# Gathered rows of an expert-choice layer: sample rows fetched for two experts at a time, and their transposes set between the down matmuls

## What is computed

```python
logits = jnp.einsum('nd,de->en', hf, w_router)
aff = jax.nn.softmax(logits, axis=0)
gate, idx = lax.top_k(aff, cap)          # cap = 128 prompt rows, 64 sample rows
xg = hf[idx]
a = jnp.einsum('ecd,edf->ecf', xg, w_gate)
b = jnp.einsum('ecd,edf->ecf', xg, w_up)
out = jnp.einsum('ecf,efd->ecd', jax.nn.silu(a) * b, w_down) * gate[..., None]
y = jnp.zeros_like(hf).at[idx.reshape(-1)].add(out.reshape(-1, D))
```

## Time and profile before

| | |
|---|---|
| time, median of three executions | 2801.92 us (2797.81 to 2806.22) |
| profiled execution, span from the first to the last instruction | 2798.9 us |
| TensorE matmuls busy | 2615.8 us, 93% |
| VectorE busy | 1852.2 us, 66% |
| ScalarE busy | 1398.5 us, 50% |
| GpSimd busy | 391.0 us, 14% |
| mean granted TensorE clock | 0.966 |

### The profile page before, as it was taken

How to read it: one execution, slowest core, us unless ns; L and a number is a source line. 1 busy time by engine, 2 the same in 40 slices (tenths; PEclk the granted TensorE clock), 3 DMA queues, 4 the chain that set the end, 5 groups by cost and what they waited for, 6 DMA issues and landing times.

```text
span 2798.9 us, 41956 instructions
## 1 busy us (share of the span) xinstructions
PE 2615.8 (93%) x15956; PEld 2371.6 (85%) x15956; DVE 1852.2 (66%) x2211; ACT 1398.5 (50%) x1751; POOL 391.0 (14%) x344
## 2 busy tenths in 40 slices
PE   6979789997995599999999999999999999999997
PEld 5877678986784599898898998989989899898996
DVE  4876889986435566576665766756657566575664
ACT  4224355666312255465564554645546455465553
POOL 2081793000000101010010100101101011010000
PEclk8999999999997799999999999999999999999998
DMA  4112000002233468687686876868768678686773
GB/s 137 41 45 85 16 1 1 1 1 90 100 113 105 134 220 248 212 255 220 228 249 210 260 220 223 252 210 256 229 216 254 210 239 245 216 257 209 236 241 110
DMA packets 347982, 475.45 MB, mean 170 GB/s; under 512 B 10112, under 2 KB 301312, under 8 KB 347776
## 3 DMA queue, kind: packets, MB, share of 16 engines
q1 hardware_dynamic: 340736, 449.22, 49.7%
q0 software_dynamic: 7168, 25.17, 3.8%
HBM read 449.19 MB, written 25.17 MB: 169 GB/s over the span
## 4 chain that ended last, share of the span: by engine, by line
PE 87%; DVE 5%; POOL 3%; ACT 2%; issue 2%; DMA 1%; ACTq 0%; POOLq 0%; DVEq 0%
PE psum L1385 29%; PE psum L1387 13%; PE psum L1149 8%; PE psum L1151 8%; PE psum L1150 8%; PE psum L1263 5%; PE psum L1402 4%; PE psum L1403 4%; PE psum L1250 2%; PE psum L1238 2%; PE psum L1368 1%; POOL qn L448 1%; DVE wi_lo L811 1%; PE psum L1369 1%; PE psum L1339 1%
## 5 line engine op out<-in xcount | busy, mean ns | idle before, releaser
L1069 DVE TENSOR_TENSOR w_lo<-raw,w_hi 128x2048 fp32r<-128x2048 f32 x384 | 880.0, 2292 | 517.6 <-ACT w_hi L689 515.7
L1385 PE MATMUL psum<-xgT,w_hi 128*128 128x384 f32 x4096 | 1167.9, 359 | 3.4 <-issue 3.4
L1387 PE MATMUL psum<-xgT,w_lo 128*128 128x192 f32 x4096 | 1026.1, 251 | 0.0
L689 ACT CAST w_hi<-raw 128x2048 fp32r<-128x2048 f32 x384 | 733.3, 1910 | 356.8 <-PE psum L1403 356.8
L1387 PEld LDWEIGHTS psum<-xgT,w_lo 128*128 128x128 f32 x4096 | 783.4, 191 | 0.7
L1385 PEld LDWEIGHTS psum<-xgT,w_hi 128*128 128x128 f32 x4096 | 770.0, 188 | 4.2 <-issue 3.5
L486 POOL DMA_INDIRECT out_dram<-o_p,put_p x16 | 25.7, 1609 | 1568.7 <-ACT o_s L728 1568.7
L784 DVE SCALAR_TENSOR_TENSOR conv<-conv,colp 128x1024 f32<-128x1024 f32 (+1 forms) x210 | 234.0, 1114 | 4.0
L1149 PE MATMUL psum<-w_hi,hid_st 128*128 128x512 f32 x512 | 207.7, 406 | 0.0
L1151 PE MATMUL psum<-w_hi,hid_st 128*128 128x512 f32 x512 | 205.8, 402 | 0.0
L1150 PE MATMUL psum<-w_lo,hid_st 128*128 128x512 f32 x512 | 205.7, 402 | 0.0
(11 more groups left out here) (186 smaller groups left out, 3544.0 us busy)
## 6 DMA issues: line engine op xcount, KB each, us to landing
raw<-in_w_gate_dram SPq DMA_DIRECT2D x128, 1024.0 KB, 5.4
raw<-in_w_up_dram SPq DMA_DIRECT2D x128, 1024.0 KB, 5.4
raw<-in_w_down_dram SPq DMA_DIRECT2D x128, 1024.0 KB, 5.0
wi_raw<-in_w_in_dram SPq DMA_DIRECT2D x56, 256.0 KB, 3.8
out_dram<-x SPq DMA_DIRECT2D x12, 512.0 KB, 2.6
h_rows<-h SPq DMA_DIRECT2D x12, 512.0 KB, 2.8
xin<-in_x_prompt_dram SPq DMA_DIRECT2D x8, 512.0 KB, 3.6
wo_raw<-in_w_out_dram SPq DMA_DIRECT2D x8, 512.0 KB, 6.4
```

The lines of the kernel that those rows point to most:

```text
L689: act.copy(w_hi[:, j % SPLIT_SLOTS, :], raw[:, j % RAW_SLOTS, :]).then_inc(e_hi, 1)
L1069: dve.tensor_tensor(w_lo[:, j % SPLIT_SLOTS, :], raw[:, j % RAW_SLOTS, :], w_hi[:, j % SPLIT_SLOTS, :].bitcast(F32), ALU.subtract).then_in ...
L1385: pe.matmul(bank[:, 0:2 * CAP], w_hi[:, slot, w0:w0 + P], xgT[:, k, :], start=(k == 0), stop=False, skip_group_check=True)
L1387: last = pe.matmul(bank[:, 0:CAP], w_lo[:, slot, w0:w0 + P], xgT[:, k, 0:CAP], start=False, stop=(k == KD - 1), skip_group_check=True)
```

## The change

Sample rows are gathered for experts 2i and 2i+1 together: `rows_sg` and `cur_sg` hold 128 row numbers, `xg_s` is 128 rows high, and one indirect DMA (`gather_pair`) serves two experts. Prompt rows are gathered for each expert as before. `xgT` has a half for each expert of the pair. A turn into an odd expert transposes the eight prompt blocks alone; a turn into an even expert transposes eight prompt blocks and eight sample blocks of 128x128, which hold the rows of both experts of the pair. On TensorE the transposes of a turn stand singly or in twos behind each group of five down matmuls, over chunks 17 and 18, and the waits for the gathered rows stand ahead of chunk 17's matmuls. ScalarE and VectorE do their part behind step 21 in place of 20; in turns into even experts it is two instructions each. To treat the two kinds of expert apart, the loops of ScalarE, VectorE, GpSimd and TensorE now hold two experts and run 7 times.

```diff
+TURN_AT, TURNED_AT = 17, 21
...
-            xg_s = in_region(re_, "xg_s", [CAP_S, D], F32)
+            xg_s = in_region(re_, "xg_s", [2 * CAP_S, D], F32)
...
-            xgT = in_region(re_, "xgT", [P, KD, 2 * CAP], F32R)
+            xgT = in_region(re_, "xgT", [P, 2, KD, 2 * CAP], F32R)
...
+            gather_pair(0)
+            with pool.Fori(0, NE // 2 - 1) as i:
+                pool.wait_ge(xg_T, 2 * i + 1)
+                gather(2 * i + 1)
+                gather_pair(i + 1)
+                scatter(2 * i)
+                pool.wait_ge(xg_T, 2 * i + 2)
+                gather(2 * i + 2)
+                scatter(2 * i + 1)
...
-            def gathered_high(e):
+            def gathered_high(e, half):
 
                 act.wait_ge(xg_T, e + 1)
-                act.copy(xgT[:, :, 0:CAP].rearrange("p (a b) c -> p a b c", a=4),
-                         psum[:, 0:4, 0:2 * CAP].rearrange("p a (b c) -> p a b c", b=2)).then_inc(xg_h, 1)
+                last = act.copy(xgT[:, half, :, 0:CAP_P], gathered_prompt())
+                if half == 0:
+                    last = act.copy(xgT[:, :, :, CAP_P:CAP], gathered_sample())
+                last.then_inc(xg_h, 1)
...
-            def gathered_T(e):
-
-                pe.wait_ge(gathered, 32 * e + 32)
+            def turn_ready(e, i):
+
+                pe.wait_ge(gathered, 16 * e + 16)
+                if i is not None:
+                    pe.wait_ge(gathered_s, 16 * i + 16)
                 pe.wait_ge(g_sum, e * PAIRS)
                 pe.wait_ge(u_sum, e * PAIRS)
-                for k in range(KD):
-                    c0 = k % 2 * CAP
-                    pe.transpose(psum[:, k // 2, c0:c0 + CAP_P], xg_p[:, k * P:(k + 1) * P], ident[:, :])
-                    last = pe.transpose(psum[:, k // 2, c0 + CAP_P:c0 + CAP], xg_s[:, k * P:(k + 1) * P],
-                                        ident[0:CAP_S, 0:CAP_S])
-                last.then_inc(xg_T, 1)
...
+            def turn_block(k, with_sample):
+
+                last = pe.transpose(gathered_prompt()[:, k, :], xg_p[:, k * P:(k + 1) * P], ident[:, :])
+                if with_sample:
+                    last = pe.transpose(psum[:, 2 + k // 4, k % 4 * P:(k % 4 + 1) * P], xg_s[:, k * P:(k + 1) * P], ident[:, :])
+                return last
...
+                        if turn is not None and TURN_AT <= j < TURN_AT + 2:
+                            k = 4 * (j - TURN_AT) + 2 * i + half
+                            turned = turn_block(k, turn == 0)
+                            if k == KD - 1:
+                                turned.then_inc(xg_T, 1)
...
+            with pe.Fori(0, NE // 2 - 1) as i:
+                late(2 * i, 0, 1)
+                early(2 * i + 1, 1)
+                late(2 * i + 1, 1, 0, i + 1)
+                early(2 * i + 2, 0)
+            late(NE - 2, 0, 1)
+            early(NE - 1, 1)
+            late(NE - 1, 1, None)
```

More of the change, by code:

```diff
@@ L739, in step, with late, expert @@
                     hid_high(e, c // 2)
-            def late(e, last):
+            def late(e, turn):
                 for j in range(TURN, EC):
                     step(e, j)
-                    if j == 20 and not last:
-                        gathered_high(e + 1)
-            act.sem_inc(o_ok, 1)
-            act.wait_ge(proj, TILES)
-            for j in range(SPLIT_SLOTS):
-                step(0, j, first=True)
[L751 to L755, removed]
+                    if j == TURNED_AT and turn is not None:
+                        gathered_high(e + 1, turn)
+            def expert(e, turn):
+                late(e, turn)
                 for j in range(TURN):
@@ L760, in _ @@
                 out_rows(e)
-            late(NE - 1, True)
+            act.sem_inc(o_ok, 1)
+            act.wait_ge(proj, TILES)
+            for j in range(SPLIT_SLOTS):
+                step(0, j, first=True)
+            gathered_high(0, 0)
+            for j in range(SPLIT_SLOTS, TURN):
+                step(0, j)
+            with act.Fori(0, NE // 2 - 1) as i:
+                expert(2 * i, 1)
+                expert(2 * i + 1, 0)
+            expert(NE - 2, 1)
+            late(NE - 1, None)
             out_low(NE - 1)
@@ L1119, in step, with late, expert @@
                     hid_low(e, c // 2)
-            def late(e, last):
+            def late(e, turn):
                 for j in range(TURN, EC):
                     step(e, j)
[L1124 to L1134, removed]
+                    if j == TURNED_AT and turn is not None:
+                        gathered_low(e + 1, turn)
+            def expert(e, turn):
+                late(e, turn)
                 gates_of(e)
@@ L1139, in _ @@
                         out_add(e)
-            late(NE - 1, True)
+            dve.sem_inc(o_add, 1)
+            for j in range(SPLIT_SLOTS):
+                step(0, j)
+            gathered_low(0, 0)
+            for j in range(SPLIT_SLOTS, TURN):
+                step(0, j)
+            with dve.Fori(0, NE // 2 - 1) as i:
+                expert(2 * i, 1)
+                expert(2 * i + 1, 0)
+            expert(NE - 2, 1)
+            late(NE - 1, None)
             gates_of(NE - 1)
@@ L1373, in chunk @@
-            def chunk(e, j):
-                slot = j % SPLIT_SLOTS
-                pe.wait_ge(e_lo, e * EC + (j + 1))
[L1376 to L1403, removed]
-                last.then_inc(e_used, 1)
@@ new lines, in down @@
+            def down(e, j, turn=None, pair=None):
+                slot, jj = j % SPLIT_SLOTS, j - 2 * PAIRS
+                pe.wait_ge(e_lo, e * EC + (j + 1))
+                if jj == 0:
+                    pe.wait_ge(o_ok, 2 * e + 1)
+                pe.wait_ge(h_lo, 2 * (e * PAIRS + (jj + 1)))
+                if turn is not None and j == TURN_AT:
+                    turn_ready(e + 1, pair)
+                for i in range(2):
+                    st = hid_st[:, 2 * jj + i, :]
+                    first, end = jj == 0 and i == 0, j == EC - 1 and i == 1
+                    for half in range(2):
+                        w0 = i * D + half * 512
+                        hi, lo = w_hi[:, slot, w0:w0 + 512], w_lo[:, slot, w0:w0 + 512]
+                        product3(psum[:, 4 + half, :], st[:, 0:CAP_P], st[:, CAP + CAP_S:2 * CAP], hi, lo, first, end)
+                        both = st[:, CAP_P:CAP + CAP_S]
+                        pe.matmul(psum[:, 6 + half, :], both, hi, start=first, stop=False)
+                        last = pe.matmul(psum[:, 6 + half, :], both, lo, start=False, stop=end)
+                        if turn is not None and TURN_AT <= j < TURN_AT + 2:
[3 more added lines that the diff above has]
+                                turned.then_inc(xg_T, 1)
+                last.then_inc(e_used, 1)
@@ new lines, in early, with late @@
+            def early(e, half):
+                for j in range(TURN):
+                    gate_up(e, half, j)
+            def late(e, half, turn, pair=None):
+                for j in range(TURN, 2 * PAIRS):
+                    gate_up(e, half, j)
+                for j in range(2 * PAIRS, EC):
+                    down(e, j, turn, pair)
+            turn_ready(0, 0)
+            for k in range(KD):
+                last = turn_block(k, True)
+            last.then_inc(xg_T, 1)
+            early(0, 0)
```

70 lines of the change are left out of this document (41 added, 29 removed).

## The result

The changed kernel takes 2776.8 us (median of four, 2772.9 to 2780.7), the kernel before 2802.1 us. The ratio is 0.991, with a 95% interval of 0.9893 to 0.9927: faster by 25 us, 0.9%. Forecast were 44 us less, 2757.8, with a range of 2746 to 2775, which the measured time misses by 1.8 us. The profiled execution of the changed kernel has a span of 2778.2 us, 20.7 less than that of before; its four executions stand in two pairs, 2772.9 and 2773.3, 2780.3 and 2780.7, and the profiled one belongs to the longer pair, so the sum further down closes on the two spans and not on the medians.

A forecast was written before the change was run, and what follows sets the result against it. TensorE was taken to bound the expert stage. Turn transposes -36.8, clock drops -13.3, stage start +1 and longer loop +5 gave -44.1 us, from 2801.9 to 2757.8 us, range 2746 to 2775.

The forecast's parts named there:

- What bounds, and the price of a transpose: Expert stage: TensorE bounds; at turns each 128x128 transpose costs 0.11 us in place of 0.23, -36.8 us in all.
- The clock behind the turn: TensorE's half clock behind nine of 15 turns goes away with the run of 16 transposes, 1.48 us each: -13.3 us.
- The start: Start of the expert stage, once: later sample gather +2, transposes -2.5, copies +1.1; sum +0.6, taken as +1 us.
- the sample gather: At the stage's start: issued later (+0.7) and fetching 128 rows, together +2 us, bounds 0 and 4.
- The other two terms: At the stage's start: 16 transposes at half clock, -2.5 us, and copies ahead of the first product, +1.1 us.
- The longer loop: TensorE's two-expert loop body may need an instruction fetch at each of 7 jumps back, 0.7 us each: +5 us.
- rival B: TensorE's jump back is dear: 2.8 us exposed each, up to 10 us more from the clock; 2773 to 2783, chance 0.10.
- Its clock term: In the dear-jump rival: idle time drops TensorE's clock at each jump, up to 10 us more (7 x 1.48).
- The lead of 2.6 us: TensorE's sequencer takes the branch 2.6 us before chunk 7 ends, hiding that much of a fetch; held against the dear jump.

The follow-up runs named there:

- the grouped order: Kernel before with each turn's eight 128-row transposes first, then the eight 64-row ones, in one run: 2754.4 us, ratio 0.9832.
- the full blocks in one run: Kernel before, one expert per body, sample block made 128 rows high with 64 rows of zeros, 16 transposes in one run: 2756.6 us, ratio 0.9841.

## Why the prediction was wrong

**What bounds, and the price of a transpose: right.** 0.11 us each, as taken from the projection stage. The length of an expert without a jump and without a drop of the clock says the same: 113.93 before, 111.83 with a turn into an even expert, and 111.15 into an odd one (111.17 in the changed kernel, 111.12 to 111.17 with the loop written out). That saves 2.8 and 2.1 us; eight and seven of them are 37.0 us, against 36.8. The reason that was given, blocks of two heights in turn, was an inference from the code; the grouped order and the full blocks in one run show it.

**The clock behind the turn: right in size, half right in cause.** All nine drops, like the one at 1149.1 us with a granted clock of 0.50, are gone, 13.3 us. That they come from the run in one piece is shown: cut into twos, even with the dearer blocks of two heights in turn, it drops nothing. But a run of transposes as such does no harm: with full or grouped blocks it is 1.7 us long and the clock stays at all 15 turns, where the old run of 3.7 us dropped it at nine. No run of 3.7 us with blocks of one height was tried, so whether its length or the 16 changes of height in it do the harm is not told apart. Spreading was not needed beside full blocks in the kernel with one expert per body; the changed kernel without its spreading was not run.

**The start: wrong, small.** +1 was said, -1.6 came. The step that failed is the sample gather, said to have its rows in place 2 us later; they were there 1.3 us sooner, counted from the row numbers. Before, the two copies of row numbers took 2.06 and 2.25 us, both ahead of the first gather. Now the first gather goes out 2.2 us sooner, and the second copy, behind it, takes 1.2; why it is shorter is not shown. The other two terms held: the transposes took 3.4 us in place of 5.7 (-2.3, said was -2.5), and from the first copy to the first product it was 1.1 longer, as said.

**The longer loop: this is the step that failed.** The mechanism and the place were named, and the term was mis-sized: +5 was taken, +31.3 measured. It went wrong in three places. The fetch was priced as one packet of 1.1 us plus a little, 3.3 us from the branch to the next instruction; it is 4.7 to 5.4. The packet itself is as short as was said, 0.9 to 1.7 us, but it starts only 2.0 to 2.8 us behind the branch, and the branch ends another 1.1 to 1.5 us behind the packet. The clock was left out of the forecast's own sum and given to rival B, though the text held that idle time might drop it; it makes nearly half of the cost. And there are six jumps and not seven. Rival B, 2773 to 2783 with a chance of 0.10, is what happened. Its 2.8 us of idle time for a jump is what was measured, but that is luck: it came from the 5.4 us in which 1 MB of weights lands, and no instruction packet has to do with that. Its clock term, 1.48 a jump, was too low, 2.4 were measured, and the seventh jump that does not exist makes up for a part of it. The lead of 2.6 us that was held against it is real (2.3 to 2.4 by the last matmul's start), and was already in that figure. That the doubled body no longer stays deserved more weight than a chance of one in ten: its consequence was cheap to work out, and no row of before showed a body of 2800 instructions that stays.

**The sum after the fact.** -37.0 - 13.3 - 1.6 + 31.3 = -20.6 us, and the two spans differ by 20.7. The medians differ by 25.3; the shorter executions of the changed kernel have no trace that would say where they are shorter.

**The better version.** The changed kernel with TensorE's loop written out, 2746.8 us, 1.9% under before. A kernel of one expert per body with its shapes grouped reaches 2754.4 by two lines and no pairs at all.

## What to carry to other kernels

Look at a transpose's neighbours before its size: keep all blocks of one height together, since each change between 128 and 64 rows cost 0.14 us here and a full-height block only 0.11. Before a loop body on TensorE is made longer, count its instructions with the weight loads and waits, and look whether the instruction queue is silent in the loop: if it is, and the new body is not sure to stay so, price every jump at the idle time plus the clock behind it (5.2 us here), or write the loop out. An idle gap of TensorE can cost more than its length: 16.6 us of them made 31.3 here.

## What was not expected of the hardware

Writing TensorE's loop out was free: 72 packets were fetched in a straight line without a single gap. A body of 1623 instructions ran without fetching and one of 1759 fetched again at every jump, 14 times 4.1 to 6.3 us. The same kind of jump waited 5.0 us in one program and 6.3 in another, for packets that mostly took about 1 us each, and its gap hardly shrank when TensorE had 1.5 us more in its queue.
